# Values stationary for the last query tile of a hybrid decoder block, with side work in other half steps

## The reference

```python
s_sel = jnp.einsum('bghqd,bgqnld->bghqnl', qi, k_sel) * scale
p_sel = softmax(where(m_sel, s_sel, NEG))
o_sel = jnp.einsum('bghqnl,bgqnle->bghqe', p_sel, v_sel)
...
o = g[0] * o_cmp + g[1] * o_sel + g[2] * o_win
```

## Time and profile before

| | |
|---|---|
| median of 3 runs | 695.2 us (694.86 to 695.87) |
| the profiled execution | 695.04 us, span 693.2 us |
| TensorE busy | 680.8 us, 98% of the span |
| weight loads of TensorE | 569.8 us, 82% |
| VectorE, ScalarE, GpSimd busy | 331.3, 226.0, 187.4 us |
| mean granted clock of TensorE | 0.997 |

### The profile page before, as it was taken

How to read it: one execution, slowest core, us unless ns; L and a number is a source line. 1 busy time by engine, 2 the same in 40 slices (tenths; PEclk the granted TensorE clock), 3 DMA queues, 4 the chain that set the end, 5 groups by cost and what they waited for, 6 DMA issues and landing times.

```text
span 693.2 us, 9147 instructions
## 1 busy us (share of the span) xinstructions
PE 680.8 (98%) x3653; PEld 569.8 (82%) x3653; DVE 331.3 (48%) x572; ACT 226.0 (33%) x384; POOL 187.4 (27%) x95
## 2 busy tenths in 40 slices
PE   7999999999999999999999999999999999999996
PEld 6888889887787878888988888888888888888885
DVE  4888898754688774626213531101000049533126
ACT  3636342240333433325423322222222122332224
POOL 2000000000000001050254455444444338455521
PEclk9999999999999999999999999999999999999998
DMA  9998978520000002760154545433432213331003
GB/s 310 354 334 297 337 277 299 194 84 32 1 1 1 1 2 74 233 179 1 31 154 127 169 129 151 122 91 92 128 116 92 91 61 122 99 113 62 1 1 122
DMA packets 74538, 88.10 MB, mean 127 GB/s; under 512 B 3112, under 2 KB 57600, under 8 KB 74368
## 3 DMA queue, kind: packets, MB, share of 16 engines
q1 hardware_dynamic: 73184, 85.31, 38.1%
q0 software_dynamic: 416, 1.08, 0.5%
q10 hardware_dynamic: 896, 1.12, 0.5%
HBM read 85.41 MB, written 2.10 MB: 126 GB/s over the span
## 4 chain that ended last, share of the span: by engine, by line
PE 93%; DVE 2%; DMA 1%; issue 1%; ACT 1%; SPq 1%; POOLq 0%; POOL 0%; DVEq 0%; ACTq 0%
PE ps L1257 13%; PE ps L1259 13%; PE ps L1258 13%; PE ps L1691 12%; PE ps L1693 12%; PE ps L1692 12%; PE ps L1428 5%; PE ps L1485 1%; DMA early<-in_w_ada 1%; PE ps L1377 1%; PE ps L1564 1%; PE ps L1403 1%; PE ps L1279 1%; PE ps L1471 1%; DVE acc L781 1%
## 5 line engine op out<-in xcount | busy, mean ns | idle before, releaser
L442 POOL TENSOR_TENSOR wl<-raw,wh 128x1024 fp32r<-128x1024 f32 x66 | 172.3, 2615 | 203.4 <-ACT wh L491 203.3
L1691 PE MATMUL ps<-hTh,wh 128*128 128x512 f32 (+1 forms) x384 | 143.6, 374 | 0.0
L1693 PE MATMUL ps<-hTh,wl 128*128 128x512 f32 (+1 forms) x384 | 142.6, 371 | 0.0
L1692 PE MATMUL ps<-hTl,wh 128*128 128x512 f32 (+1 forms) x384 | 142.6, 371 | 0.0
L491 ACT ACTIVATE wh<-raw 128x1024 fp32r<-128x1024 f32 x94 | 97.1, 1039 | 109.6 <-PE ps L1693 74.0
L1187 DVE TENSOR_TENSOR act<-ps,sg 128x512 f32<-128x512 f32 x22 | 15.2, 692 | 195.1 <-PE ps L1693 195.1
L1257 PE MATMUL ps<-wh,hTh 128*128 128x512 f32 (+2 forms) x232 | 89.5, 386 | 0.0
L1259 PE MATMUL ps<-wh,hTl 128*128 128x512 f32 (+2 forms) x232 | 86.4, 372 | 0.0
L1258 PE MATMUL ps<-wl,hTh 128*128 128x512 f32 (+2 forms) x232 | 86.3, 372 | 0.0
L1692 PEld LDWEIGHTS ps<-hTl,wh 128*128 128x128 f32 x384 | 72.3, 188 | 12.9 <-issue 0.5
L1691 PEld LDWEIGHTS ps<-hTh,wh 128*128 128x128 f32 x384 | 72.3, 188 | 12.8 <-issue 0.5
(11 more groups left out here) (198 smaller groups left out, 887.4 us busy)
## 6 DMA issues: line engine op xcount, KB each, us to landing
raw<-in_w_ada SPq DMA_DIRECT2D x32, 512.0 KB, 5.1
raw<-in_w_ff_gate SPq DMA_DIRECT2D x22, 512.0 KB, 3.9
raw<-in_w_ff_up SPq DMA_DIRECT2D x22, 512.0 KB, 3.7
raw<-in_w_ff_down SPq DMA_DIRECT2D x22, 512.0 KB, 3.2
raw<-in_w_in SPq DMA_DIRECT2D x20, 512.0 KB, 8.2
early<-in_w_ada SPq DMA_DIRECT2D x16, 512.0 KB, 9.6
raw<-in_w_out SPq DMA_DIRECT2D x8, 512.0 KB, 3.5
xs<-in_x SPq DMA_DIRECT2D x4, 512.0 KB, 5.2
```

The lines of the kernel that those rows point to most:

```text
L442: pool.tensor_tensor(lo, raw[:, slot, 0:n], hi.bitcast(F32), ALU.subtract).then_inc(w_lo2, 1)
L1691: mm(o, hi[:, ks], hTh[:, k, c0:c1], start=k == 0, stop=False)
L1692: mm(o, hi[:, ks], hTl[:, k, c0:c1], start=False, stop=False)
L1693: ins = mm(o, lo[:, ks], hTh[:, k, c0:c1], start=False, stop=k == KT - 1)
```

## The change

For the last query tile (branches 6 and 7, value steps 12 to 19) V is the stationary operand and PT streams: one float32 matmul of 512 columns for each group, 64 output partitions each, both groups in bank 2, giving the transposed output of four heads. Without the column of ones, the denominators are made otherwise: GpSimd adds the PT buffers of a branch over its key steps (`weight_sum`, six additions of 128x1024), and after the attention four matmuls with one column of ones as stationary operand (`den_sums`) put the column sums on partitions 0, 32, 64 and 96 of bank 3. The transposed outputs and the denominators are copied by ScalarE and transposed back on TensorE (4 + 4 + 4 transposes), and VectorE divides, gates and adds them. These go between the first output units, whose order changes; for the last tiles four units stand together (`FILL`). The exponentials from step 14 on also wait for sums on GpSimd that read the buffer they write, and the reload of x waits for `den_sums`. The powers of the retention norm are placed among the sums in GpSimd's list. Side work takes other half steps, two more output scalings come before `mix_low(3)`, and the minima of branch 1 come before the compressed scores of tile 0 on VectorE.

```diff
 STEPS = STEP0[-1]
-PAIR_AT = {1: [(4, 0)], 3: [(4, 1)], 6: [(4, 2)], 7: [(4, 3)], 10: [(5, 0)], 12: [(5, 1)], 13: [(5, 2)], 14: [(5, 3)], 15: [(6, 0)], 16: [(6, 1)], 19: [(6, 2)], 22: [(6, 3)], 24: [(7, 0)], 26: [(7, 1)], 29: [(7, 2)], 30: [(7, 3)]}
-MAX_AT = {0: 2, 2: 3, 9: 4, 17: 5, 23: 6, 31: 7}
+PAIR_AT = {1: [(4, 0)], 4: [(4, 1)], 6: [(4, 2)], 7: [(4, 3)], 10: [(5, 0)], 12: [(5, 1)], 13: [(5, 2)], 14: [(5, 3)], 15: [(6, 0)], 16: [(6, 1)], 19: [(6, 2)], 22: [(6, 3)], 24: [(7, 0)], 25: [(7, 1)], 27: [(7, 2)], 29: [(7, 3)]}
+MAX_AT = {0: 2, 2: 3, 9: 4, 17: 5, 23: 6, 30: 7}
 CS_AT = {9: 2, 21: 3}
-CT_AT = {15: 2, 23: 3}
+CT_AT = {15: 2, 24: 3}
 CO_AT = {0: 1, 16: 2, 25: 3}
-RS_AT = {8: (1, 0), 11: (1, 1), 18: (2, 0), 21: (2, 1), 27: (3, 0), 28: (3, 1)}
-RV_AT = {2: [(0, 0), (0, 1)], 10: [(1, 0)], 13: [(1, 1)], 20: [(2, 0)], 22: [(2, 1)], 29: [(3, 0)], 33: [(3, 1)]}
-SQ_AT = {3: 0, 13: 1, 22: 2, 35: 3}
-NORM_AT = {5: 0, 14: 1, 23: 2, 36: 3}
+RS_AT = {8: (1, 0), 11: (1, 1), 18: (2, 0), 21: (2, 1), 26: (3, 0), 28: (3, 1)}
+RV_AT = {2: [(0, 0), (0, 1)], 11: [(1, 0)], 13: [(1, 1)], 20: [(2, 0)], 22: [(2, 1)], 29: [(3, 0)], 36: [(3, 1)]}
+SQ_AT = {3: 0, 13: 1, 22: 2, 37: 3}
+NORM_AT = {5: 0, 14: 1, 23: 2, 38: 3}
 M_AT = {7: 0, 18: 1, 27: 2}
-OUT_AT = {16: 0, 18: 1, 27: 2, 34: 3}
+OUT_AT = {16: 0, 18: 1, 29: 2, 35: 3}
 SLOTS = 2 * (STEPS + 1)
+WIDE = GROUPS - 2
+WIDE0 = STEP0[WIDE]
+SUMMED = [n for x in (WIDE, WIDE + 1) for n in range(STEP0[x] + 1, STEP0[x + 1])]
+FILL = 4
...
         KTl = at("KTl", [P, 2, T], F32R, R + 20)
+        QTf = at("QTf", [P, 2, HPG, T], F32, R)
...
         mcol = at("mcol", [P, 2, P], F32, 111)
+        OT = at("OT", [P, 2, T], F32, 40)
+        denR = sqj
...
         rgt = small("rgt", [P, NH])
+        rgw = small("rgw", [P, 2 * NH])
...
             return hTf[:, p, :, (TT - 1) * P:T].rearrange("p (a j) q -> p a j q", a=2)
+        def sums(b):
+            return QTf[:, b].rearrange("p h (t q) -> p t h q", q=P)[:, 0:NG]
+        def weights(n):
+            return PT[:, n % 2].rearrange("p g (h q) -> p g h q", h=HPG)
...
         mx_ps, mx_min, mx_T, mb_ok, st_ps, p_exp, pv, o_read = (sem(n) for n in ("mx_ps", "mx_min", "mx_T", "mb_ok", "st_ps", "p_exp", "pv", "o_read"))
+        p_sum, oT_ok, den_ps, den_ok, denT_ps, den_read, o_T = (sem(n) for n in ("p_sum", "oT_ok", "den_ps", "den_ok", "denT_ps", "den_read", "o_T"))
...
             return g, n - STEP0[g]
+        def sum_count(n):
+            return SUMMED.index(n) + 1
...
                     sp.wait_ge(cs_ps, TT)
+                    sp.wait_ge(den_ps, 1)
...
             pool.memset(mcol[:, :, :], 0.0).then_inc(mcol_set, 1)
-            for i in range(TT):
-                power(N_RET + i, yss[:, :])
+            def weight_sum(n):
+                x, j = step(n)
+                acc_ = sums(x % 2)
+                pool.wait_ge(p_exp, NG * (n + 1))
+                if j > 1:
+                    pool.wait_ge(p_sum, sum_count(n) - 1)
+                pool.tensor_tensor(acc_, weights(n - 1) if j == 1 else acc_, weights(n), ALU.add).then_inc(p_sum, 1)
+            for n in range(SLOTS):
+                if n - 1 in SQ_AT:
+                    power(N_RET + SQ_AT[n - 1], yss[:, :])
+                if n % 2 == 0 and n // 2 in SUMMED:
+                    weight_sum(n // 2)
...
                         a.wait_ge(pv, n - 1)
+                    if n >= WIDE0 + 2:
+                        a.wait_ge(p_sum, sum_count(n - 2 if n - 2 in SUMMED else n - 1))
...
                              ACT.Copy).then_inc(mix_hi, 1)
+            def out_copy(b):
+                a.wait_ge(pv, STEP0[WIDE + b + 1])
+                a.activation(OT[:, b, :], ps[:, 2, :], ACT.Copy).then_inc(oT_ok, 1)
+            def den_copy():
+                a.wait_ge(den_ps, 1)
+                a.wait_ge(r_sq, TT)
+                a.activation(denR[:, :], ps[:, 3, :], ACT.Copy).then_inc(den_ok, 1)
...
             for n in range(SLOTS):
+                if n == 2 * STEP0[WIDE + 1] + 2:
+                    out_copy(0)
...
                     high(U0_OUT + OUT_AT[n])
+            out_copy(1)
+            den_copy()
...
                                 r.unsqueeze(3).broadcast_to([P, NG, HPG, DH]), ALU.mult).then_inc(o_read, 1)
+            def den_gates():
+                d.wait_ge(denT_ps, 1)
+                den = ps[:, 3, :].rearrange("p (h c z) -> p c h z", h=HPG, z=CP)[:, :, :, 0]
+                d.reciprocal(rgw[:, :].rearrange("p (c h) -> p c h", h=HPG), den).then_inc(den_read, 1)
+                d.wait_ge(den_read, 1)
+                then(d.tensor_tensor(rgw[:, :], rgw[:, :], gates[:, TT - 1, NH:3 * NH], ALU.mult))
+            def add_wide(b):
+                d.wait_ge(o_T, 2)
+                d.wait_ge(b_mix, WIDE + b)
+                r = rgw[:, b * NH:(b + 1) * NH].rearrange("p (g h) -> p g h", g=NG)
+                d.tensor_tensor(tmpo[:, :].rearrange("p (g h e) -> p g h e", g=NG, e=DH),
+                                ps[:, 3 - b, :].rearrange("p (h g e) -> p g h e", h=HPG, g=NG),
+                                r.unsqueeze(3).broadcast_to([P, NG, HPG, DH]), ALU.mult).then_inc(o_read, 1)
...
                     max_rows(0)
-                    cmp_scores(0)
...
                         row_min(1, h)
+                    cmp_scores(0)
...
             for n in range(SLOTS):
-                if n % 2 and n // 2 in STEP0[1:]:
+                if n % 2 and n // 2 in STEP0[1:WIDE + 1]:
...
                     max_rows(MAX_AT[n])
-                if n % 2 and n // 2 in STEP0[1:]:
+                if n % 2 and n // 2 in STEP0[1:WIDE + 1]:
...
                     scale_unit(U0_OUT + OUT_AT[n + 1])
+            den_gates()
+            for b in range(2):
+                add_wide(b)
+                mix_branch(WIDE + b)
+            for u in (U0_OUT + SPLIT, U0_OUT + SPLIT + 1):
+                scale_unit(u)
...
             for u in range(U0_OUT + SPLIT, U0_GU):
-                scale_unit(u)
-                if u > U0_OUT + SPLIT:
-                    low(u - 1)
-            low(U0_GU - 1)
+                low(u)
+                if u + 2 < U0_GU:
+                    scale_unit(u + 2)
...
                 ins.then_inc(pv, 1)
+            def wide_values(n):
+                x, j = step(n)
+                i, b = divmod(x, 2)
+                if j == 0:
+                    if b:
+                        pe.wait_ge(oT_ok, 1)
+                    else:
+                        pe.wait_ge(o_read, WIDE)
+                pe.wait_ge(p_exp, NG * (n + 1))
+                for g in range(NG):
+                    ins = mm(ps[g * DH:(g + 1) * DH, 2, :].rearrange("p (h q) -> p h q", h=HPG), V[:, j, b, g, 0:DH], weights(n)[:, g],
+                             start=j == 0, stop=j == i)
+                ins.then_inc(pv, 1)
+            def den_sums():
+                pe.wait_ge(p_sum, len(SUMMED))
+                for b in range(2):
+                    for g in range(NG):
+                        c = CP * (NG * b + g)
+                        ins = mm(ps[c:c + 1, 3, :].rearrange("p (h q) -> p h q", h=HPG), ones[:, 0:1], sums(b)[:, g], start=True, stop=True)
+                ins.then_inc(den_ps, 1)
+            def den_transposes():
+                pe.wait_ge(den_ok, 1)
+                for h in range(HPG):
+                    ins = pe.transpose(ps[:, 3, h * P:(h + 1) * P], denR[:, h * P:(h + 1) * P], ident)
+                ins.then_inc(denT_ps, 1)
+            def out_transposes(b):
+                pe.wait_ge(oT_ok, 2)
+                if b == 0:
+                    pe.wait_ge(den_read, 1)
+                for h in range(HPG):
+                    ins = pe.transpose(ps[:, 3 - b, h * P:(h + 1) * P], OT[:, b, h * P:(h + 1) * P], ident)
+                ins.then_inc(o_T, 1)
...
                 if n % 2 and n >= 3:
-                    values(n // 2 - 1)
+                    (wide_values if n // 2 - 1 >= WIDE0 else values)(n // 2 - 1)
...
-            wait_low(pe, U0_OUT + 1)
+            wait_low(pe, U0_OUT + FILL - 1)
...
             pe.wait_ge(mb_ok, GROUPS)
-            for k in range(2):
+            out_unit(0, 0)
+            out_unit(2, 0)
+            den_sums()
+            out_unit(0, 1)
+            out_transposes(1)
+            den_transposes()
+            out_unit(2, 1)
+            out_transposes(0)
+            for k in range(2, FILL):
...
             pe.wait_ge(o_read, GROUPS)
-            out_unit(1, 0)
-            out_unit(1, 1)
+            for k in range(FILL):
+                out_unit(1, k)
             pe.wait_ge(mix_lo, TT)
-            for k in range(KT - OUT_TAIL):
-                if k >= 2:
-                    wait_low(pe, U0_OUT + k)
-                for t in range(TT) if k >= 2 else (TT - 1,):
-                    ins = out_unit(t, k)
-                ins.then_inc(unit_used, 1)
+            for k in range(FILL):
+                out_unit(TT - 1, k).then_inc(unit_used, 1)
```

## The result

The changed kernel takes 691.86 us (median of 6 runs, 691.28 to 692.28), the kernel before in the same session 695.43 us (694.76 to 695.87): ratio 0.995, interval 0.994 to 0.9959, 3.6 us less. A second session gave 692.04 against 695.22 us, ratio 0.9952 (0.9939 to 0.9964). The forecast was 691.3 us. The profiled execution has a span of 690.1 us against 693.2, so 3.1 us of the gain are in its trace.

The account below looks back on a forecast made before the run. TensorE, busy for 98% of the span, was taken to bound the kernel. Second maximum −0.7, attention −5.5 and tail +2.5 sum to −3.7 us: forecast 691.3 us, range 690.0 to 695.6.

Parts of the forecast that it names:

- second maximum: Before the attention: branch 1's minima start earlier on VectorE, so TensorE's 0.7 us wait before the transpose goes, −0.7 us.
- values: Last query tile: eight values steps fall from 1.75 to 0.86 us each if column groups overlap fully, −7.1 us.
- (a): Attention: three values steps now stand beside full-array work, each with a new change of matmul form, +0.3 us.
- (b): Attention: scores wait for exponentials, 0.1 to 0.15 us in three places and 0.3 before the very last, +0.6 us.
- (c): Attention: retention scores (3,0) and (3,1) each wait 0.7 us for a pair's minima, replacing a 0.5 us wait, net +0.9.
- (d): Attention: compressed-part transposes leave half step 23, so scores 12 come before their block of maxima is ready, +0.1 us.
- (e): Attention: retention scores, pairs and masks follow scores in the same matmul form at more places, −0.3 us.
- tail: After the attention: denominator matmuls +1.1 us and 12 transposes +1.4 us, other new work hidden, +2.5 us.
- staggered rival: Values steps: the second group waits its turn, 1.29 us a step, so 695.4 us, no change; chance 0.12.
- Hidden, as priced: Attention: six GpSimd sums of 2.4 us stay covered by TensorE work, at step 18 4.0 against 2.5 + 1.1; 0 us.
- The rival: Attention: GpSimd sums take 3.4 us or wait for VectorE, delaying exponentials, +1 to +3 us, 693.3 us; chance 0.15.
- case without overlap: Values steps: column groups run one after the other, 1.72 us a step, denominators 3.4 us, 700.2 us; chance 0.08.

Follow-up runs that it names:

- after: The changed kernel as profiled, with no further edit: span 690.1 us, median 691.86 us.
- same_columns: The changed kernel with the second group of the eight values steps written to output partitions 0 to 63 of bank 3, the first group's array columns: 697.92 us.
- spread_high: The changed kernel with last-tile retention scores in half steps 31 and 33, values (3,0) 33, mix transposes 28, mix_low(2) 30, third and fourth output weights 32, 36: 690.12 us.
- values_33: The changed kernel with the last retention values, (3,1), back in half step 33 instead of 36: 693.05 us.
- scalings_after: The changed kernel with the scalings of the fifth and sixth output weight put back behind mix_low(3): 693.27 us.
- old_tables: The changed kernel with all tables of side work as they were before the change: 694.22 us.
- the first three spreadings: The changed kernel with last-tile retention scores in half steps 31 and 33; then mix_low(2) in 30, third output weight 31; then that weight 32: 694.9, 691.48, 691.94 us.
- spread_scores: The changed kernel with last-tile retention scores moved to half steps 31 and 33, retention values (3,0) to 33, mix transposes for tile 2 to 28: 694.9 us.
- sums_twice: The changed kernel with every sum on GpSimd made twice, the extra one into unused memory: 704.36 us.
- spread_last: The changed kernel with last-tile retention scores in half steps 31 and 33, values (3,0) 33, mix transposes 28, mix_low(2) 30, third output weight 32: 691.94 us.

## Why the prediction was right

The sum was right to 0.6 us at the median (691.3 against 691.86). Its terms, in the order of the prediction:

| term | forecast | measured in the trace |
|---|---|---|
| second maximum | −0.7 | −0.5 in after (start of scores at 221.69, before 222.21); −0.8 alone, by its time |
| values, with (a) changes of form | −7.1 + 0.3 | −6.6 |
| (b) and (c), waits | +0.6 + 0.9 | +0.3 + 0.65 |
| (d) and (e), order of the rest | +0.1 − 0.3 | +0.4, all that is left over |
| tail | +2.5 | +2.55 |
| sum | −3.7 | −3.1, the median −3.6 |

The rows of the attention are worked out from the timelines of TensorE in both traces, from the transpose of a maximum at 222.00 and 221.49 to the first output matmul, by adding for each kind of work the times from its starts to the next start, with the waits taken out: the values lines hold 21.8 us before and 15.2 after, the waits 0.5 and 1.5, all else 31.8 and 32.2. By rounding the rows add up to −3.2.

The mechanism was the one forecast, and every large term came near its size. That the sum is as near as 0.6 us is in part luck: the waits of (b) and (c) were 0.55 us too high and the order of the rest 0.6 too low, and these two misses cancel.

**Values.** The overlap was taken from row groups and holds for column groups: same_columns tells it by 5.9 us in the time and 0.85 us in a step. The forecast took a step for 0.86 us and a change of form beside it. The last two steps, in one form with nothing between them, take 2.02, so the 0.15 above 0.86 is paid by every step of column groups and is not the price of a change of form. In same_columns the last two, eight records one after the other, take 3.58 (273.14 to 276.72), 0.14 above 8 × 0.43, and so pay it once; why column groups pay it each time is not shown. This is where the values fell short: the last two gained 3.49 − 2.02 = 1.47 us and not 2 × 0.89 = 1.78. The other six gained 5.1, where 5.0 was said with (a) taken off. The staggered rival wanted 1.4 to 1.5. The Trainium skill (TensorE: Matmul & The Clock Gate, Part 3) has matmuls start and end strictly in program order. The trace does not contradict that: the four records start at 265.54 (two) and 266.02 (two), and none overtakes another. What failed is what the rival drew from it, that both records of group 0 go ahead of group 1's first: the step took a time near that of two records (0.86) and not of three (1.29). Which record belongs to which group no view here tells. The denominators, eight records in four column groups, took 0.97 us: two records deep and a change of form, as forecast (1.06), and not 3.4.

**The waits.** Those of retention scores came at both places and were 0.6 and not 0.7 us. Those for exponentials came at two places of the three, 0.16 and 0.17 us, and the 0.3 before the very last one did not. Under (d) and (e) the rest came out 0.4 us longer where 0.2 less was forecast. That row also holds what the changes of form of (a) cost on other lines, and its cause stays open, as no run takes it alone; spread_high is 1.8 us shorter than after from 243 us to the first output matmul, and its waits are only 1.3 us less, which says that the order is worth some tenths.

**GpSimd.** Hidden, as priced, by a margin of 0.5 us at step 18, where the prediction had 4.0 against 3.6. values_33 takes the cover away and finds 1.4 us where 1.5 was said. The rival had named VectorE's two-input operations as the danger, and one of them did lengthen a sum to 3.36 us; it was that of step 15, over at 260.84, and exponentials 17, which wait for it, had no scores before 261.29. The Trainium skill (SBUF — State Buffer, "SBUF: two separate sides") calls the port an exclusive lock; the 3.40 us of the scaling agree.

**The tail.** 25.35 us against 25.3. The last low part ends 23.9 us into it, where 23.6 was forecast, and has 1.46 us to spare, where 1.7 was said; scalings_after, which takes 2.4 of it, finds the 0.9 us that should remain.

The expectations for old_tables and the first three spreadings missed by one omission: a wait was followed to its engine, and not to the held operation ahead of it there, or in the queue of the engine that feeds that one.

## What to carry to other kernels

A matmul with few output partitions is worth turning around when two of them can stand in different columns of the array; look first for the price of one record of the streaming length, and make the case without overlap by one edit, as it decides the sign. When a step on the bound engine grows shorter and another engine gets new work beside it, the places of all side work have to be chosen anew: with the old tables 2.2 of 3.2 us were lost, and with better ones 1.9 more were won. Before an operation with two inputs in SBUF goes to VectorE beside GpSimd, read what stands behind it on VectorE, and then what stands behind its reader on the next engine; keep both free of what TensorE waits for.

## What the runs showed that was not expected

- The longest waits of TensorE cost more than their length. After the one of 3.0 us (spread_scores) the granted clock was 0.50, the 1.2 GHz level, for at least 3 us of work that followed, 1.6 us on top. In sums_twice, behind stretches of 4 us with 0.91 and 1.41 us of work in them, it was 0.57 and 0.69. Waits up to 1.6 us (old_tables, spread_last) left the sum of the time at what the waits explain: old_tables lost 2.2 us with 2.2 us more in its list of waits than after, values_33 1.0 with 1.2 more.
- Wherever a sum on GpSimd met one of VectorE's operations with two inputs in SBUF, they ran one after the other: the sum of 2.4 us took 3.36 behind a low part, the scaling of 1.22 us took 3.40 behind that sum, and four other scalings behind sums 2.54, 2.88, 3.39 and 3.40. An operation of 128x4 with one input in SBUF was held too, 1.42 us and not 0.17. One with its other input in PSUM was not: the decay of 251.56 in after took its 1.23 us beside the sum of 250.96.
- Column groups overlap fully for float32 matmuls of two records: 1.01 us for four records, against 1.86 in the same columns. Beyond the streaming of two records each such step pays 0.15 us, also when the next one has the same form.
